# Differential attention's weights made in their own step, and the two turning rounds on either side of the step's pieces of projection

## The reference

```python
def block(args):
    qblk, qi = args
    s = jnp.einsum('bhcqd,bhckd->bhcqk', qblk, kh).astype(jnp.float32) * scale
    mask = kidx[None, :] <= qi[:, None]
    p = jax.nn.softmax(jnp.where(mask, s, -jnp.inf), axis=-1)
    w = p[:, :, 0] - lam * p[:, :, 1]
    return jnp.einsum('bhqk,bhkv->bhqv', w, vh)
```

## Time and profile before

| what | value |
|---|---|
| median of 3 runs | 2523.24 us (2522.43 to 2524.48) |
| the profiled execution | 2524.78 us |
| its span, first to last instruction | 2523.0 us |
| mean granted TensorE clock | 0.983 |
| the 32 steps of differential attention | from about 78 to 369 us of the span |
| TensorE busy over the span | 95% |

### The profile page before, as it was taken

How to read it: one execution, slowest core, us unless ns; L and a number is a source line. 1 busy time by engine, 2 the same in 40 slices (tenths; PEclk the granted TensorE clock), 3 DMA queues, 4 the chain that set the end, 5 groups by cost and what they waited for, 6 DMA issues and landing times.

```text
span 2523.0 us, 35033 instructions
## 1 busy us (share of the span) xinstructions
PE 2396.7 (95%) x14684; PEld 1814.1 (72%) x14684; DVE 1123.6 (45%) x1494; ACT 855.1 (34%) x1468; POOL 540.0 (21%) x244
## 2 busy tenths in 40 slices
PE   7999999999999898999999999999999999999997
PEld 4767666555577776677888888888867677778885
DVE  5767654344556423443112112112342846466554
ACT  4333335556534322223113113013232522254421
POOL 2312111111120221232212221222223123223222
PEclk9999999999999999999999999999999999999999
DMA  3211101102123100111111111111221001100022
GB/s 135 66 42 45 34 31 51 34 17 101 58 67 126 34 26 17 34 42 42 50 42 51 51 43 49 50 42 54 101 73 43 25 26 34 45 26 12 3 101 75
DMA packets 37277, 126.07 MB, mean 50 GB/s; under 512 B 3856, under 2 KB 4368, under 8 KB 36752
## 3 DMA queue, kind: packets, MB, share of 16 engines
q1 hardware_dynamic: 30864, 103.30, 12.6%
q10 hardware_dynamic: 6272, 20.72, 2.2%
HBM read 114.57 MB, written 8.91 MB: 49 GB/s over the span
## 4 chain that ended last, share of the span: by engine, by line
PE 86%; DVE 8%; ACT 4%; issue 1%; ACTq 0%; POOL 0%; DVEq 0%
PE PS L179 21%; PE PS L181 21%; PE PS L180 21%; PE PS L1879 2%; PE PS L873 2%; PE PS L858 2%; PE PS L713 2%; PE PS L1117 1%; PE PS L736 1%; PE PS L1094 1%; PE PS L885 1%; PE PS L898 1%; PE PS L715 1%; PE PS L311 1%; PE PS L725 1%
## 5 line engine op out<-in xcount | busy, mean ns | idle before, releaser
L179 PE MATMUL PS<-u_r,w_hi 128*128 128x512 f32 x1280 | 521.5, 407 | 16.1 <-ACT arena L637 3.3
L181 PE MATMUL PS<-u_r,w_lo 128*128 128x512 f32 x1280 | 507.3, 396 | 0.0
L189 POOL TENSOR_TENSOR w_lo<-w_raw,w_hi 128x1024 fp32r<-128x1024 f32 x143 | 359.2, 2512 | 593.8 <-ACT w_hi L185 587.8
L180 PE MATMUL PS<-arena_r,w_hi 128*128 128x512 f32 (+1 forms) x1152 | 439.5, 382 | 0.0
L228 POOL TENSOR_TENSOR w_hi<-w_raw,const 128x1024 fp32r<-128x1024 f32 x77 | 152.2, 1977 | 1273.3 <-PE PS L179 1120.1
L179 PEld LDWEIGHTS PS<-u_r,w_hi 128*128 128x128 f32 x1280 | 241.7, 189 | 96.6 <-issue 13.9
L181 PEld LDWEIGHTS PS<-u_r,w_lo 128*128 128x128 f32 x1280 | 242.0, 189 | 57.4
L180 PEld LDWEIGHTS PS<-arena_r,w_hi 128*128 128x128 f32 x1152 | 216.9, 188 | 44.5 <-issue 0.7
L179 PE MATMUL PS<-h_r,w_hi 128*128 128x512 f32 x512 | 210.5, 411 | 4.1 <-DVE u_r L383 3.8
L179 PE MATMUL PS<-y_r,w_hi 128*128 128x512 f32 x512 | 203.9, 398 | 0.0
L181 PE MATMUL PS<-h_r,w_lo 128*128 128x512 f32 x512 | 202.9, 396 | 0.0
(11 more groups left out here) (392 smaller groups left out, 3624.4 us busy)
## 6 DMA issues: line engine op xcount, KB each, us to landing
w_raw<-in_w SPq DMA_DIRECT2D x174, 512.0 KB, 3.6
arena<-in_w SPq DMA_DIRECT2D x10, 512.0 KB, 5.5
h<-in_xT ACTq DMA_DIRECT2D x1, 4096.0 KB, 12.9
u<-parked_stream ACTq DMA_DIRECT2D x1, 4096.0 KB, 13.1
out<-arena SPq DMA_DIRECT2D x16, 256.0 KB, 2.0
parked_stream<-h ACTq DMA_DIRECT2D x6, 512.0 KB, 2.6
h<-in_xT SPq DMA_DIRECT2D x8, 256.0 KB, 7.8
h<-in_xT ACTq DMA_DIRECT2D x8, 256.0 KB, 9.5
```

Source lines behind the costliest of these rows:

```text
L179: first = pe.matmul(out, a[0], b[0], start=start, stop=False)
L180: pe.matmul(out, a[0], b[1], start=False, stop=False)
L181: return first, pe.matmul(out, a[1], b[0], start=False, stop=stop)
L189: return e.tensor_tensor(out, x, hi_part.bitcast(F), ALU.subtract)
```

## The change

It moves instructions and adds none. VectorE makes the weights of step g at the end of step g itself, behind `ada_dve`, `da_final` or `rope_dve`, instead of behind the maxima of step g+1. Where the turning of g-1 takes two rounds, TensorE does the first one ahead of the pieces of step g and the second one behind them, and ScalarE does its two copies in the same places. One round alone stays behind the pieces. The turning of step 31 stays whole; its weights are made in step 31.

```diff
-        def da_turn(pe, g):
+        def da_turn(pe, g, rds):
             t = g % NT
             pe.wait_ge(S("w_ready"), g + 1)
-            for rd in turn_rounds(g):
+            for rd in rds:
...
             da_scores(pe, g)
             if g >= 2:
                 da_values(pe, g - 2)
+            if g >= 1 and len(turn_rounds(g - 1)) > 1:
+                da_turn(pe, g - 1, [0])
             for c in da_chunks(*divmod(g, NT)):
                 chunk_pe(pe, c)
             if g >= 1:
-                da_turn(pe, g - 1)
-
-        def da_copy_turned(act, g):
-            for rd in turn_rounds(g):
+                da_turn(pe, g - 1, turn_rounds(g - 1)[-1:])
+
+        def da_copy_turned(act, g, rds):
+            for rd in rds:
...
+            if g >= 1 and len(turn_rounds(g - 1)) > 1:
+                da_copy_turned(act, g - 1, [0])
             for c in da_chunks(i, s):
                 chunk_act(act, c)
             if g >= 1:
-                da_copy_turned(act, g - 1)
+                da_copy_turned(act, g - 1, turn_rounds(g - 1)[-1:])
...
-            if g >= 1:
-                da_weights(dve, g - 1)
             if s < 3:
                 ada_dve(dve, i, s)
             if s == 4 and i > 0:
                 da_final(dve, i - 1)
             if s in (5, 6) and i + 1 < N_DA:
                 rope_dve(dve, i + 1, s - 5)
+            da_weights(dve, g)
...
-                if g == 0:
-                    da_weights(dve, DA_N - 1)
```

More of the change, by code:

```diff
@@ L865, in sb_pe @@
                 if g == 0:
-                    da_turn(pe, DA_N - 1)
+                    da_turn(pe, DA_N - 1, turn_rounds(DA_N - 1))
             if 1 <= g <= SB_ALL:
@@ L912, in sb_act @@
             if g == 0:
-                da_copy_turned(act, DA_N - 1)
+                da_copy_turned(act, DA_N - 1, turn_rounds(DA_N - 1))
             if g == 1:
```

## The result

| | before | with the change |
|---|---|---|
| median | 2523.82 us (2522.43 to 2524.48, 4 runs) | 2492.25 us (2487.95 to 2495.03, 4 runs) |
| profiled execution | 2524.78 us | 2490.04 us |
| its span | 2523.0 us | 2488.3 us |

The ratio is 0.9874, 95% interval 0.9857 to 0.9891. The direction was right.

What follows compares the result with a forecast made beforehand. TensorE, busy 95% of the span, was taken as the bound. Stalls of 16.2 us plus 6.6 us of clock, 22.8 us off the profiled 2524.78, gave 2502.0; the median, 1.54 lower, 2500.5 us, range 2494 to 2512.

Steps and rivals of the forecast that it cites:

- 11 splits: Steps 5, 6 and the next head's step 0: a piece between the rounds covers ScalarE's copy, saving 7.9 us.
- step 7: Each head's step 7: no wait for weights, second round starts 1.6 us earlier, four times, saving 6.3 us.
- step 4: Step 4 waits for weights go: 0.92 us in the first three heads, 1.1 us in the fourth, together 2.0 us.
- clock: TensorE's granted clock falls less around step 7, giving back 6.6 us of a possible 9.6 us.
- 0.72 us each: TensorE's waits between rounds for ScalarE's copy of the first: 11.5 us over 16 waits, the price used per wait.
- I take two falls left: Clock falls become fewer and shorter: two remain, each 1.5 us, so 6.6 us come back.
- The price of all four falls: Clock falls in the profile before: nine tenths of at most 10.6 us lost, so 9.6 us.
- the weights are in time for the first round everywhere: First round ahead of the piece: weights ready in time, tightest in step 5 (1.6 to 1.8 against 2.9 us); nothing counted.
- ScalarE's queue is what is late next in step 7: Step 7's second round waits about 1.05 us for ScalarE's copy, which stands behind that step's exponentials.
- the fourth head's step 5 moves its wait to the exponentials: Fourth head: step 4's turning stops waiting; step 5's scores wait about 0.9 us for the exponential instead.
- The rival of VectorE as the bound: Moved weights delay VectorE's maxima, exponentials and the scores after them: slower, 2553 us, chance 0.05.
- waits only move: ScalarE's first-round copy is late in steps 5 and 6 too, 8 waits stay: about 2513 us, chance 0.13.

Runs made afterwards that it cites:

- filler kernel: Two products of 128x512 that nobody reads, added to the kernel before in each head's step 7 while TensorE waits for weights: 2515.39 us, ratio 0.9967.

## Why the prediction was wrong

The terms, measured on the lengths of the steps. The filler kernel stands for "before without falls".

| term | predicted | measured | from |
|---|---|---|---|
| 11 splits | 7.9 | 10.7 | steps 5 and 6 of all heads 7.8; steps 0 9.50 against 10.47 in the filler kernel, three times |
| step 7 | 6.3 | 6.2 | 7.18 against 8.72, four times |
| step 4 | 2.0 | 2.6 | 0.69, 0.43, 0.43, 1.00 |
| clock | 6.6 (0 to 9.6) | 9.8 | steps 7 and 0, before against the filler kernel |
| sum | 22.8 | 29.3 | 303.98 against 274.7 us over steps and first stick-breaking step |

**The first step that failed: "0.72 us each".** I took the idle time in brackets as the price of a wait. The splits show 0.94 to 0.97 us a wait. In the second head step 6 went from 10.63 us (its scores and those of step 7 before, below) to 9.70 us (the after rows at 192.44 and 202.14), and in the kernel with only the weights moved it kept 10.64.

```profile
200.93 1.77 PE L713 MATMUL PS<-y 64*128 64x512 f32 x8
...
211.56 1.99 PE L713 MATMUL PS<-y 64*128 64x512 f32 x8
```

The reason stands in the rows: a row's idle time counts from the end of the last matmul. But a matmul that need not wait starts before the one ahead has ended: four turned tiles take 0.60 us where one takes 0.27, so they start 0.11 us apart. In the filler kernel the second round at 216.02 starts 1.35 us after the first at 214.67, of which 0.44 is four tiles at that distance; 0.91 us are lost where the bracket says 0.69. That is 0.2 us a wait, over the 11 splits and the first three steps 4 some 3 us, and it was to be had from the trace before.

**The second: "I take two falls left".** None was left in two profiles of the change, one in the third. The price of all four falls, 9.6 us, worked out as nine tenths of half the busy time (21.25 us at PEclk 0.50), was right for that profile: the filler kernel gives 9.8 on the steps and 9.2 on the medians. What I misjudged is how much the shorter waits would do. Four gaps with 1.86 and 0.69 us of waits had four falls; with one wait of 1.72 us two short ones; with one of 1.26 us none or one. I priced the middle of an unknown and the end was the truth. With the change the first round's four transposes also stand in the gap (205.94); what shorter waits and moved transposes did each is not separated, since no run shows transposes by themselves.

These two are 2.8 + 0.6 and 3.2 us, the whole difference in the steps. Some 2 us more went outside them (31.2 us between the spans of equal pace, 29.5 in the steps); what brought these is not shown.

Two small slips in the working change nothing. Step 7's four times 1.6 us are 6.4, not 6.3. And in the second head the fall at 221.2 begins 1.4 us after the second wait has ended (219.80), not 0.8.

**What was right.** The direction and its reason; that the weights are in time for the first round everywhere; that ScalarE's queue is what is late next in step 7, and the length that leaves it (6.2 against 6.3); that the fourth head's step 5 moves its wait to the exponentials (1.1 us, about 0.9 foreseen); that VectorE keeps 2.4 us before the maxima of step 7 (2.25). The rival of VectorE as the bound fell. The hold by GpSimd that spoke for it did happen, at 215.36: 2.30 us for 128 columns beside a GpSimd operation that began at 215.19 and took 2.39, where the same operation of the first head, at 87.35 with GpSimd idle, took 0.34 us. It cost nothing, since the next maxima still found VectorE waiting (1.93 us). That waits only move was wrong for the whole change; with the split alone a wait did move, to the one for the weights and not, as that rival had it, to a late copy.

## What to carry to other kernels

Price a wait of TensorE by start-to-start times against a place without the wait, not by the idle time in a row; and where a gap is followed by a fall of the clock, add up to half of TensorE's busy time in the fall (here 9.8 us of 10.6), since filling or shortening the gap may take the fall away, as it did here: four falls before, none with the gap filled, none to two with it shortened. The split around other work paid here only with its input ready a step earlier (alone it cost 22.8 us in the steps): move the producer first. Then ask what the second half waits for, and whether an idle engine can do that copy.

## What the runs showed that I had not expected

Useless work in a gap made the kernel 9.2 us faster (ratio 0.9967, 0.9954 to 0.998): it stood where TensorE waited anyway, step 7 stayed 8.72 us long, and the clock held behind it (PEclk 1.00 from 76 to 366 us).

Products of the same matmuls, back to back at full clock with nothing waiting, have two paces: 133 of them in the 30 us shown of the change, 130 before. Over 3200 matmuls that is about 749.5 or 756.3 us, in twelve profiles never in between. The quick pace showed in all three profiles of the change and in the one with only the split, the slow pace in the eight others, among them a kernel that differs from the change by 15 needless waits alone, and two that hold the whole change. Two attempts to bring it about in the kernel before by the number of instructions failed. What sets it stays open; it makes a difference of up to 7 us between executions possible that no term of this change explains.
